# First cache pages and tables asked for later, and value loads in four portions, in the step kernel of a hybrid decoder

## The chip, the cores and the metric

The kernel runs on one core of one Trainium2 chip. The metric is the device time of one execution in microseconds (us). The core has five engines that run side by side and wait for each other by semaphores: TensorE (PE, matrix products), VectorE (DVE), ScalarE (ACT), GpSimd (POOL) and SyncE (SP). SP, ACT and POOL also issue transfers (DMAs), which 16 DMA engines carry out.

## What is computed

One layer of a decoder step for a prompt of 512 tokens (after 16 learned meta tokens) and for 8 sampled sequences of 8 new tokens with 1024 past positions each. The part that matters here, from the reference:

```python
xn = rmsnorm(hs, norm1[l])
qa, ka, va, qkv_b, z, b_raw, a_raw = project(xn, w_in[l], q_norm[l], k_norm[l])
kpast = cache_k[l][page_table].reshape(db, n_past, HA, 2, DQK)
vpast = cache_v[l][page_table].reshape(db, n_past, HA, DVA)
oa = diff_attn_core(qa, k_all, v_all, qpos, kpos, ..., lam, slopes)       # 4 heads
gq, gk, gv, gg, gbeta, conv_new = gdn_inputs(qkv_b, state_conv[l], ...)   # causal conv, 4 taps
s_new, ob = gdn_chunk(state_ssm[l].astype(f32), gq, gk, gv, gg, gbeta)    # 4 heads
hs = hs + merge_heads(oa, ob, z, ...)
hs = hs + peer_ffn(rmsnorm(hs, norm2[l]), ...)                            # 128 experts a token
```

The prompt goes through the same functions. All values are 32-bit floats.

## The kernel before

The 592 tokens lie in five tiles: four of 128 prompt tokens and a last one of 80 rows (64 sample rows, 16 meta rows), which comes first (`ORDER`).

**Projection units.** The 3584 columns of the input projection are cut into seven sections of 512. A unit (`UNITS`) is one tile times one section: 8 products of 128x512, in four quarters of two. Units 0 to 2 are v, k and q of the sample tile; units 3 to 7 are the first conv section over all five tiles, 8 to 12 the second, and so on. The weights of a unit come in four pieces of 512 KB, into a ring of six buffers (`w_loads`, L668): piece 6 and later each wait for the quarter that used the buffer, so piece 15, the last quarter of unit 3, waits for the second quarter of unit 2.

**Conv steps.** Unit 3+m feeds conv step m. ACT copies the unit's result out (L989, which also frees its bank) and stores it to DRAM, SP loads its rows back shifted by the four taps (`conv_inputs`, L693 to L696), DVE multiplies and adds (L1397, L1399, L1400), ACT takes SiLU and squares (L1090, L1100). For steps 0 to 9 DVE then writes a mean square (L1407), POOL turns it into a norm factor (`conv_rstd`, L869), and DVE multiplies by it (L1412 or L1414), which SP spills (L705).

**Past attention.** The 8 sequences go in four pairs. For a pair, SP loads 16 pages of keys (`key_loads`, L815, 256 KB each) and POOL 16 pages of values (`value_loads`, L906). The buffers of values are `vtok`, `kT` and two parts of `zone`, four pages each, and are free again when the values of the pair in front are used up (`s_dpv`). The chain of pair p is: scores on PE (L2018, L2023), bias adds on DVE (L1591, L1592), maximum (L1595), exponential on ACT (L1214), factors on DVE (L1599 to L1601), weights turned on PE (L2033), copied by ACT (L1219), values weighted on PE (L2045, L2048). `small_columns` (L1774, L1776) are sixteen narrow products in the middle of the first pair's chain: they use the banks that its scores stand in, so they wait for the bias adds (`s_dadd`), and for the tables.

**What sets the order.** Every engine runs a queue in program order. That order is written by streams: each piece of work yields a due time, and `advance` always takes the one that is due first. Due times are no times of the chip; they order instructions. For the early part all are `early_at(k)`, directly or by `unit_at(n)` (10.4 a unit for units 4 to 14), `conv_at(m)` (unit 3+m, its length, plus 13), `past_at(p, k)` and `gdn_at(u, k)`. So the units are the filler between the steps of the pairs' chains, and a due time that is moved changes which instruction stands ahead of which.

```python
def advance(streams, until):
    while min(s.due for s in streams) <= until:
        s = min(streams, key=lambda s: s.due)
        s.due = next(s.steps, NEVER)
```

After the last unit the kernel routes each prompt tile to experts and gathers their rows (`peer_uv`), from about 500 us to the end. The functions that the change touches, with the line numbers of the profile:

## Time and profile before

| what | value |
|---|---|
| median of 3 runs | 2113.99 us (2113.4 to 2118.76) |
| the profiled execution | 2111.61 us, span 2109.9 us |
| PE, DVE, ACT, POOL busy | 81%, 63%, 38%, 37% of the span |
| mean traffic over the span | 369 GB/s |
| PE waits in the first 560 us for DVE L1601 (ahead of L2033) | 20.2 us in 4 waits, the longest 8.8 |
| PE waits there for weight pieces (ahead of L1763) | 19.8 us in 8 waits, the longest 13.3 |

The span is the time from the first to the last instruction of the profiled execution; the device time contains 1.7 us more. Views that cut the span into stretches give for each the busy time of each engine, the TensorE clock that was granted (1.00 is full speed, 2.4 GHz, 0.50 is 1.2 GHz) and the share of time in which the DMA engines were busy (it can come out a little above 1). A timeline lists instructions or merged runs of them in order; square brackets tell how long the engine was idle ahead of a row and what released it. The trace has two records for each product of `bank<-sb_w,sb_xnT`, the program's order has one row entry for it: x20 in a timeline are ten products.

### The profile page before, as it was taken

The numbers are of one execution on the slowest core, as the hardware profiler recorded it, in microseconds if no ns is written. First come the engines' busy times: TensorE is split into PE (matmuls) and PEld (weight loads), VectorE is DVE, ScalarE is ACT, GpSimd is POOL, SyncE is SP. The second block draws the span as 40 slices with busy tenths as digits, with TensorE's granted clock in tenths as the row PEclk, the third lists the DMA queues.
The fourth block names the chain that finished last, engine by engine and source line by source line (L and its number), as shares of the span: only waits on it lengthen the run. The fifth ranks groups of instructions, "written<-read, shape, count | busy, mean of one in ns | idle before, by whom it ended". The sixth has DMA issues, their size and how long they took to land.

```text
span 2109.9 us, 20560 instructions
## 1 busy us (share of the span) xinstructions
PE 1713.4 (81%) x6211; PEld 863.1 (41%) x6211; DVE 1333.7 (63%) x3023; ACT 801.0 (38%) x2371; POOL 778.8 (37%) x704
## 2 busy tenths in 40 slices
PE   5889799988897878889797879978895567776877
PEld 1333364547453445445344535443551223442211
DVE  1343514344797657887665888865787866669554
ACT  1342321231545523563533455453243332323433
POOL 3123010111344543436334444634433554444442
PEclk9889899999999999999898999999898879888999
DMA  9999633128899999999999999999999999999997
GB/s 331 325 348 340 223 116 112 48 100 325 354 426 415 427 428 428 426 419 413 426 407 427 427 426 403 419 414 426 427 426 411 427 428 427 428 426 427 427 427 318
DMA packets 137479, 779.61 MB, mean 369 GB/s; under 512 B 14863, under 2 KB 23839, under 8 KB 59784
## 3 DMA queue, kind: packets, MB, share of 16 engines
q0 software_dynamic: 88384, 621.30, 70.6%
q1 hardware_dynamic: 45504, 149.69, 18.9%
q10 hardware_dynamic: 3480, 7.31, 0.9%
q8 instruction: 49, 0.80, 0.1%
q14 instruction: 62, 0.51, 0.1%
HBM read 762.27 MB, written 16.26 MB: 369 GB/s over the span
## 4 chain that ended last, share of the span: by engine, by line
PE 36%; DMA 32%; DVE 16%; ACT 7%; issue 4%; POOL 2%; SPq 1%; POOLq 1%; ACTq 0%; another core or an unknown queue 0%; DVEq 0%
DMA sb_uv<-in_peer_uv,sb_eidx 28%; PE bank L2145 17%; DVE sb_uv L1742 7%; PE bank L1763 6%; PE bank L2112 3%; PE bank L2080 2%; DMA sb_hres<-pre_conv 1%; ACT sb_diag L1321 1%; DVE sb_hres L1716 1%; POOL sb_uv L948 1%; ACT sb_ew L1314 1%; ACT L1310 1%; PE bank L1877 1%; PE bank L1889 1%; DVE sb_top L1643 1%
## 5 line engine op out<-in xcount | busy, mean ns | idle before, releaser
L2145 PE MATMUL bank<-sb_uv,sb_diag 128*128 128x512 f32 (+1 forms) x1860 | 960.1, 653 | 308.5 <-ACT sb_diag L1321 296.5
L948 POOL DMA_INDIRECT sb_uv<-in_peer_uv,sb_eidx x576 | 685.0, 1189 | 903.1 <-PE bank L2145 695.4
L1742 DVE CUSTOM_DVE_ANT_0 sb_uv<-sb_uv,sb_xn 128x1024 f32<-128x1024 f32 x576 | 698.9, 1221 | 326.2 <-DMA sb_uv<-in_peer_uv,sb_eidx 316.4
L2145 PEld LDWEIGHTS bank<-sb_uv,sb_diag 128*128 128x128 f32 (+1 forms) x1860 | 338.5, 197 | 806.2 <-ACT sb_diag L1321 470.2
L1310 ACT ACTIVATE sb_gel<-sb_h 128x1 f32<-128x1 f32 x576 | 116.3, 202 | 796.4 <-DVE sb_h L1742 790.0
L1763 PE MATMUL bank<-sb_w,sb_xnT 128*128 128x512 f32 (+1 forms) x560 | 270.9, 626 | 32.7 <-DMA sb_w<-in_w_sections 19.8
L1321 ACT ACTIVATE sb_diag<-sb_stay,sb_ew 128x128 f32<-128x128 f32 (+1 forms) x465 | 183.2, 394 | 48.5 <-PE bank L2145 5.3
L1314 ACT ACTIVATE sb_ew<-sb_gel,sb_gate 128x1 f32<-128x1 f32 x576 | 169.7, 295 | 19.8
L2112 PEld LDWEIGHTS bank<-sb_rT,sb_zone 128*128 128x128 f32 x1280 | 156.8, 196 | 28.3 <-issue 28.3
L1763 PEld LDWEIGHTS bank<-sb_w,sb_xnT 128*128 128x128 f32 (+1 forms) x560 | 99.5, 189 | 157.3 <-issue 121.9
L2112 PE MATMUL bank<-sb_rT,sb_zone 128*128 128x128 f32 x1280 | 157.8, 279 | 1.8 <-issue 1.8
L1716 DVE SCALAR_TENSOR_TENSOR sb_hres<-sb_uv,sb_ew,sb_hres 128x1024 f32<-128x1024 f32 x111 | 142.2, 1281 | 0.2 <-ACT sb_ew L1314 0.2
L2080 PE MATMUL bank<-sb_zone,sb_rT 128*128 128x512 f32 x160 | 71.4, 593 | 2.0 <-ACT sb_rT L1247 2.0
L884 POOL TENSOR_TENSOR sb_rstd<-sb_ms,sb_minus_half 128x8 f32<-128x8 f32 (+1 forms) x10 | 16.4, 1642 | 104.4 <-DVE sb_ms L1425 104.3
L1742 DVE DVE_READ_ACCUMULATOR2_ANT sb_h<- 128x1 f32 x576 | 47.2, 82 | 0.0
L2080 PEld LDWEIGHTS bank<-sb_zone,sb_rT 128*128 128x128 f32 x160 | 30.2, 190 | 40.3 <-issue 40.3
L1397 DVE TENSOR_TENSOR sb_xin<-sb_xin,sb_taps 128x2048 f32<-128x2048 f32 (+1 forms) x8 | 18.3, 2289 | 39.3 <-DMA sb_xin<-pre_conv 39.3
L1310 ACT ACT_TABLE_LOAD x33 | 42.3, 1283 | 0.6
L1647 DVE FIND_INDEX8 sb_tix<-sb_top,sb_score 128x8 uint32<-128x128 f32 x144 | 38.4, 284 | 0.0
L1643 DVE MAX8 sb_top<-sb_score 128x8 f32<-128x128 f32 x144 | 31.4, 279 | 6.9 <-ACT sb_score L1282 6.9
L1489 DVE TENSOR_TENSOR sb_X<-sb_X,bank 128x256 f32<-128x256 f32 (+1 forms) x36 | 14.7, 408 | 29.7 <-PE bank L1889 28.1
L1877 PEld LDWEIGHTS bank<-sb_X,sb_MT 128*128 128x128 f32 (+1 forms) x184 | 23.0, 186 | 16.6 <-issue 16.2
(335 smaller groups left out, 1518.0 us busy)
## 6 DMA issues: line engine op xcount, KB each, us to landing
sb_zone<-in_w_route SPq DMA_DIRECT2D x20, 2304.0 KB
sb_w<-in_w_sections SPq DMA_DIRECT2D x40, 512.0 KB, 8.7
sb_zone<-in_w_mixer SPq DMA_DIRECT2D x10, 2048.0 KB
sb_uv<-in_peer_uv,sb_eidx POOLq DMA_INDIRECT x576
sb_sS<-in_cache_kT SPq DMA_DIRECT2D x32, 256.0 KB, 4.5
sb_zone<-in_cache_v POOLq DMA_DIRECT2D x32, 256.0 KB, 5.9
sb_zone<-in_cache_kT SPq DMA_DIRECT2D x32, 256.0 KB, 3.7
sb_hres<-pre_conv SPq DMA_DIRECT2D x6, 1024.0 KB
```

The lines of the kernel that those rows point to most:

```text
L948: nc.gpsimd.indirect_dma_start(uv[:, m % RING, :], None, i["peer_uv"], bass.IndirectOffsetOnAxis(ap=eidx[:, t % 2, n:n + 1], axis=0)).then ...
L1310: nc.scalar.activation(G["gel"][:, at], G["h"][:, at], ACT.Gelu).then_inc(s_dg, 1)
L1314: nc.scalar.activation(G["ew"][:, at], G["gel"][:, at], ACT.Copy, scale=gate[:, t % 2, n:n + 1]).then_inc(s_dg, 1)
L1321: nc.scalar.activation(G["diag"][:, d % DIAGS, 0:cols], eye, ACT.Copy, scale=G["ew"][:, at]).then_inc(s_dg, 1)
L1643: n_top = count.inc(nc.vector.max(top[:, q, k:k + 8], sets[q]), s_tk)
L1716: nc.vector.scalar_tensor_tensor(hres[:, t % 2, :], uv[:, m % RING, D:2 * D], G["ew"][:, m % 8:m % 8 + 1], hres[:, t % 2, :], ALU.mult, AL ...
L1742: nc.vector.tensor_tensor_reduce(out=uv[:, m % RING, 0:D], in0=uv[:, m % RING, 0:D], in1=xn2[:, t % 2, :], scale=1.0, scalar=0.0, op0=ALU. ...
L1763: ins = nc.tensor.matmul(bank[b][0:rows, :], lhsT=xT(t)[:, kk, :], rhs=F["w"][:, piece % PIECES, kk % 2, :], start=kk == 0, stop=kk == KC - 1)
L1877: ins = nc.tensor.matmul(bank[PAIR_BANKS[pair][0]][0:rows, n * rows:(n + 1) * rows], lhsT=B["MT"][0:rows, lv % 2, h, 0:rows], rhs=B["X"][0 ...
L2080: ins = nc.tensor.matmul(bank[6 + half][:, :], lhsT=R["rT"][:, k, :], rhs=weights_half(half)[:, k, :], start=k == 0, stop=k == KC - 1)
L2112: ins = nc.tensor.matmul(bank[6 + g % 2][:, 128 * s:128 * s + 128], lhsT=weights_half(g)[:, k, 128 * s:128 * s + 128], rhs=R["rT"][:, k, : ...
L2145: ins = nc.tensor.matmul(bank[half][0:rows, :], lhsT=G["diag"][:, d % DIAGS, 0:rows], rhs=uv[:, m % RING, D + 512 * half:D + 512 * half + ...
```

## The change

Only due times change, and the value loads get four due times in place of two:

- all four pairs: `past_at(p, k)` is 78 + 30 p + k in place of 66 + 32 p + k, so the first pair's steps come 12 later, the second's 10, the third's 8, the fourth's 6;
- the first pair's keys are due at 47 and 56 in place of 38.5 and 39.5, its values at 60, 64, 69 and 73 in place of 42 (two) and 51 (two);
- values of later pairs are due at 30, 32, 34 and 36 behind the pair in front, in place of 27 and 28;
- the biases are due at 62 in place of 46, the narrow weights and the two tables at 64, 66 and 70 in place of 54, 56 and 59;
- L1412/L1414 of a conv step and its spill come 1.1 later; `gdn_at` of the first two tiles starts 3 and 2 later.

```diff
 def gdn_at(u, k):
     if u < 2:
-        return early_at((208, 302)[u] + (2.06, 2.15)[u] * k)
+        return early_at((211, 304)[u] + (2.06, 2.15)[u] * k)
...
 def past_at(p, k):
-    return early_at(66 + 32 * p + k)
+    return early_at(78 + 30 * p + k)
...
-                    yield early_at(54)
+                    yield early_at(64)
                     sp.dma_start(F["wba"][:, :, :], i["w_ba"]).then_inc(s_tables, 16)
...
                 def past_biases():
-                    yield early_at(46)
+                    yield early_at(62)
...
                 def key_loads(p):
                     for half in range(2):
-                        yield past_at(p - 1, 5 + 2 * half) if p else early_at(38.5 + half)
+                        yield past_at(p - 1, 5 + 2 * half) if p else early_at(47 + 9 * half)
...
                 def value_loads(p):
                     for half in range(2):
-                        yield past_at(p - 1, 27 + half) if p else early_at(42 + 9 * half)
+                        yield past_at(p - 1, 30 + 4 * half) if p else early_at(60 + 9 * half)
                         if p == 0 and half == 0:
                             pool.wait_ge(s_vecs, 112)
                         for seq in range(2):
+                            if seq:
+                                yield past_at(p - 1, 32 + 4 * half) if p else early_at(64 + 9 * half)
...
-                        yield conv_at(m) + 8.5
+                        yield conv_at(m) + 9.6
                         dve.wait_ge(s_brs, m + 1)
```

Two lines are added, so in the changed kernel every line behind L896 has a number higher by 2.

**SP's queue, at the first key pages.** Here `sb_w` are the weight pieces, L638 a tile of x, L723 the stores of the sample tile's keys, L811 the reading of a page number, with which each load of a page begins. Before:

```order
L640 DMA sb_xin<-in_x_sample 64x1024
L641 DMA sb_xin<-in_meta_tokens 16x1024
L668 DMA sb_w<-in_w_sections 128x1024 x11
L811 TENSOR_LOAD sb_pages
L811 ISA x2
```

Now:

```order
L668 DMA sb_w<-in_w_sections 128x1024 x12
L723 DMA out_k_sample<-sb_qkn 64x512
L723 DMA out_k_prompt<-sb_qkn 16x512
L668 DMA sb_w<-in_w_sections 128x1024
L638 DMA sb_hres<-in_x_prompt 128x1024
L668 DMA sb_w<-in_w_sections 128x1024
L811 TENSOR_LOAD sb_pages
```

Piece 15, three stores and loads and pieces 16 and 17 now stand ahead of the first key page; before, eight key pages stood ahead of piece 15. The second eight key pages, which stood behind piece 15, now stand behind conv step 0's rows (L693, L694), and the biases and tables behind those.

**PE's queue, around the first pair's scores.** L1763 are the units, L2018 and L2023 the scores, L1774 and L1776 the small columns, L2033 the turned weights of the pair. Before:

```order
L1793 MATMUL bank<-sb_stay,sb_qkn 128x80 x8
L1763 MATMUL bank<-sb_w,sb_xnT 128x512 x10
L2018 MATMUL bank<-sb_sS,sb_qt 32x512 x8
L1763 MATMUL bank<-sb_w,sb_xnT 128x512 x2
L2018 MATMUL bank<-sb_zone,sb_qt 32x512 x8
L2023 MATMUL bank<-sb_kT,sb_qt 32x64 x8
L1763 MATMUL bank<-sb_w,sb_xnT 128x512 x8
L1774 MATMUL bank<-sb_xnT,sb_wba 8x512 x2
```

Now (line numbers higher by 2):

```order
L1795 MATMUL bank<-sb_stay,sb_qkn 128x80 x8
L1765 MATMUL bank<-sb_w,sb_xnT 128x512 x18
L2020 MATMUL bank<-sb_sS,sb_qt 32x512 x8
L1765 MATMUL bank<-sb_w,sb_xnT 128x512 x4
L2020 MATMUL bank<-sb_zone,sb_qt 32x512 x8
L2025 MATMUL bank<-sb_kT,sb_qt 32x64 x8
L1765 MATMUL bank<-sb_w,sb_xnT 128x512 x6
L1776 MATMUL bank<-sb_xnT,sb_wba 8x512 x2
```

From the turns of the sample tile to the small columns there stood 20 unit products, now 28; up to the end of the first pair's values 26, now 34. Between the pairs it is 24 and 24 (first to second), 24 and 24, then 24 and now 20.

**DVE's queue, between conv step 0 and the first pair's bias adds.** L1407, L1412 and L1397 to L1400 belong to conv steps, L1339 scales the last tile of turned x, L1346 is a mean square of a tile of x. Before:

```order
L1407 TENSOR_SCALAR sb_bms<-sb_bss 80x4
L1339 TENSOR_TENSOR sb_xnT<-sb_xnT,sb_gain 128x1024
L1591 TENSOR_TENSOR sb_pot<-bank,sb_bias_past 128x512 x2
L1592 TENSOR_TENSOR sb_pot<-bank,sb_oT 128x64
L1412 SCALAR_TENSOR_TENSOR sb_kqv<-sb_kqv,sb_brs 80x512
```

Now (line numbers higher by 2):

```order
L1409 TENSOR_SCALAR sb_bms<-sb_bss 80x4
L1341 TENSOR_TENSOR sb_xnT<-sb_xnT,sb_gain 128x1024
L1414 SCALAR_TENSOR_TENSOR sb_kqv<-sb_kqv,sb_brs 80x512
L1348 TENSOR_SCALAR sb_ms<-sb_ss 128x1 x2
L1399 TENSOR_TENSOR sb_hres<-sb_hres,sb_taps 128x2048
L1401 TENSOR_TENSOR sb_hres<-sb_hres 128x1024
L1402 TENSOR_TENSOR sb_hres<-sb_hres 128x512
L1593 TENSOR_TENSOR sb_pot<-bank,sb_bias_past 128x512 x2
```

The adds now stand behind the norm of step 0 and all of conv step 1. In POOL's queue the norm factors L869 stood one ahead of the second pair's 16 value loads (besides the sample tile's) and three behind; now it is three ahead and three behind. The third pair's loads had one sample-tile and two prompt-tile factors behind them and now have two behind them; of the fourth pair's, four stand ahead of the last factor and twelve behind it, where all 16 stood ahead of the last two. The first pair's four portions now have one L860 or L869 or both between them, and the third portion stands behind the L860 that waits for the DVE row L1346 behind conv step 0.

## Rows read from the trace of the kernel before

**Rows 1.** Stretches: span of each, then busy us (instructions), clock, DMA share, GB/s

```profile
25.00:59.00 34.00, 16.74 (x32) 4.78 (x33) 7.05 (x14) 1.90 (x3) 12.01 (x18) 0.81 1.03 396
59.00:104.30 45.30, 41.22 (x196) 16.58 (x195) 17.25 (x30) 19.61 (x51) 6.06 (x6) 0.95 0.92 316
104.30:150.80 46.50, 37.06 (x158) 15.64 (x157) 19.74 (x32) 18.56 (x53) 11.70 (x19) 0.85 0.96 352
150.80:193.40 42.60, 39.37 (x185) 17.47 (x185) 18.11 (x24) 16.24 (x48) 11.69 (x19) 0.92 0.89 308
193.40:238.40 45.00, 35.94 (x151) 14.70 (x150) 21.41 (x23) 11.95 (x30) 11.20 (x19) 0.85 0.77 285
260.00:440.00 180.00, 172.88 (x763) 98.33 (x762) 64.20 (x117) 39.48 (x93) 17.16 (x13) 0.99 0.28 92
```

**Rows 2.** Timeline of PE, start: start us, us, what, records, [idle before, releaser]

```profile
26.60 5.51 PE L1763 MATMUL bank<-sb_w,sb_xnT 128*80 128x512 f32 x12 [2.39 <-DMA sb_w<-in_w_sections]
...
55.52 3.70 PE L1763 MATMUL bank<-sb_w,sb_xnT 128*80 128x512 f32 x4 [13.34 <-DMA sb_w<-in_w_sections]
...
62.62 10.52 PE L1763 MATMUL bank<-sb_w,sb_xnT 128*128 128x512 f32 x20 [2.06 <-issue]
```

**Rows 3.** Timeline of SP's queue

```profile
5.31 23.56 SPq L668 DMA_DIRECT2D sb_w<-in_w_sections  x11
35.36 6.28 SPq L815 DMA_DIRECT2D sb_sS<-in_cache_kT  x8
41.68 0.44 SPq L668 DMA_DIRECT2D sb_w<-in_w_sections  x1
```

**Rows 4.** The page's DMA issues: operation, count, KB each, median us to landing

```profile
sb_w<-in_w_sections SPq DMA_DIRECT2D x40, 512.0 KB, 8.7
...
sb_zone<-in_cache_v POOLq DMA_DIRECT2D x32, 256.0 KB, 5.9
```

**Rows 5.** The chain of waits in the first 520 us: start us, us, what

```profile
41.68 13.80 DMA sb_w<-in_w_sections
```

**Rows 6.** Timeline of PE, the four pairs

```profile
86.58 1.03 PE L1774 MATMUL bank<-sb_xnT,sb_wba 128*8 128x512 f32 x4 [0.53 <-DVE sb_pot L1592]
...
92.81 2.00 PE L2033 MATMUL bank<-sb_pot 128*128 128x64 f32 x16 [0.16 <-DVE sb_pot L1601]
...
135.81 3.68 PE L2033 MATMUL bank<-sb_pot 128*128 128x64 f32 x16 [8.78 <-DVE sb_pot L1601]
...
139.83 6.38 PE L1763 MATMUL bank<-sb_w,sb_xnT 128*128 128x512 f32 x8
...
181.51 2.52 PE L2033 MATMUL bank<-sb_pot 128*128 128x64 f32 x16 [3.23 <-DVE sb_pot L1601]
...
209.20 8.85 PE L1763 MATMUL bank<-sb_w,sb_xnT 128*128 128x512 f32 x20
226.06 3.67 PE L2033 MATMUL bank<-sb_pot 128*128 128x64 f32 x16 [8.01 <-DVE sb_pot L1601]
```

**Rows 7.** Timeline of DVE, conv steps and bias adds

```profile
77.63 2.29 DVE L1397 TENSOR_TENSOR sb_xin<-sb_xin,sb_taps 80x2048 f32<-80x2048 f32 x1 [11.53 <-DMA sb_xin<-pre_conv]
...
85.11 1.28 DVE L1591 TENSOR_TENSOR sb_pot<-bank,sb_bias_past 128x512 f32<-128x512 f32 x2
...
127.12 1.28 DVE L1591 TENSOR_TENSOR sb_pot<-bank,sb_bias_past 128x512 f32<-128x512 f32 x2
...
256.33 2.29 DVE L1397 TENSOR_TENSOR sb_hres<-sb_hres,sb_taps 128x2048 f32<-128x2048 f32 x1 [4.30 <-DMA sb_hres<-pre_conv]
```

**Rows 8.** Timeline of POOL, the second pair's values

```profile
104.97 2.29 POOL L906 DMA_DIRECT2D sb_vtok<-in_cache_v  x4 [4.76 <-PE bank L2048]
...
121.26 1.04 POOL L869 TENSOR_TENSOR sb_brs<-sb_bms,sb_minus_half 128x4 f32<-128x4 f32 x1
```

**Rows 9.** The DMA queues from 42 to 56 us: packets, MB, share of 16 engines

```profile
q1 hardware_dynamic: 1618, 3.21, 61.7%
q0 software_dynamic: 702, 2.27, 42.1%
```

More of the change, by code:

```diff
@@ L647, in tables_loads @@
                     sp.dma_start(st("ident"), stay_table[:, 0:128]).then_inc(s_ident, 16)
-                    yield early_at(54)
+                    yield early_at(64)
                     sp.dma_start(F["wba"][:, :, :], i["w_ba"]).then_inc(s_tables, 16)
-                    yield early_at(56)
+                    yield early_at(66)
                     sp.dma_start(stay[:, 128:], stay_table[:, 128:]).then_inc(s_tables, 16)
-                    yield early_at(59)
+                    yield early_at(70)
                     sp.dma_start(F["early"][:, :], early_table).then_inc(s_tables, 16)
@@ L698, in spills @@
                 def spills(m):
-                    yield conv_at(m) + (9.5 if m < 2 * NT else 4.7)
+                    yield conv_at(m) + (10.6 if m < 2 * NT else 4.7)
                     sec, n = divmod(m, NT)
```

## The prediction

> **What bounds the kernel now.** I read the stretches first [rows 1]. From 260 us on PE is busy 172.88 of 180 us and the DMA engines 0.28 of the time; there and later the change moves only a few products. Before 238.4 us it is the other way round: the DMA engines are at 1.03 up to 59 us and at 0.92, 0.96, 0.89 and 0.77 in the stretches that end with each pair's values, while PE idles and its clock falls to 0.81 and 0.85. So the early part is bound by two things at once: transfers nearly all the time, and PE waits at single places. PE's timeline names the places. One is at 42.18 us: PE waits 13.34 us for a weight piece [rows 2]. The others are waits for DVE L1601 ahead of L2033, 8.78, 3.23 and 8.01 us in pairs two to four [rows 6]. Each costs more than itself. Behind the first wait a quarter of a unit takes 3.70 us; at full clock a record takes 8.85 / 20 = 0.44 us, a quarter 1.8 [rows 2, 6]. A gap that closes at PE before 240 us moves everything behind it, since PE is full afterwards.
>
> **The sum, against the profiled execution (2111.61 us).**
>
> A, the weight piece. SP issues piece 15 at 41.68, straight behind eight key pages that took it from 35.36, and it lands 13.80 us later [rows 3, 5]. It needs only the second quarter of unit 2, which is two thirds through the run that starts at 26.60: about 30.3 [rows 2]. In the new order the piece stands with its eleven forerunners, so it is issued at about 30.4 and lands between 30.4 + 8.7 (the median) and 30.4 + 13.8: 39.1 to 44.2 [rows 4, 5]. PE comes for it at 55.52 - 13.34 = 42.18. The wait falls to 0 to 2 us; I take 0.3, a gain of 13, since the value pages that shared the engines are gone too. The clock adds 3.70 - 1.8 for that quarter and 10.52 - 8.85 for the next run [rows 2, 6]: 3.5. Of the 2.39 us ahead of 26.60 and the like I take 1. A = 17.5 (11 to 21).
>
> B, the first pair. DVE gets conv step 0's rows at 77.63 and does the adds at 85.11, 7.5 us later [rows 7]. Now the adds stand behind the norm of step 0 and all of step 1. From the rows at time T: about 4.3 for step 0 on DVE, 0.6 for the tile's factor on POOL, 4.1 for the third portion of values (a quarter of the 16.3 us from 104.97 to 121.26), only then 1.0 for L869 of step 0, then on DVE 0.7 for L1412, 4.3 for step 1 and 2.6 for the adds: 17.6, and 1.4 for seven handovers, T + 19 [rows 7, 8]. T itself moves with A: 77.6 - 17.5 = 60.1, so the small columns can start at 79.3. PE reaches them earlier: units restart at 62.62 - 17.5 = 45.1, then 28 products of 0.885 and 4.2 us of scores: 74.1 [rows 2, 6]. A new wait of 5.2 us, where 0.53, 0.16 and about 1 us stood [rows 6]. B = -4 (0 to -10). Behind PE there only units are queued; DVE, ACT and POOL don't wait for them in this stretch. The fourth portion of values is issued by T + 17.6 = 77.7 and lands 5.9 later [rows 4]; PE wants it after 91. Tables and biases are issued about as long ahead of their use as before. Both cost nothing while that cover of some 7 us stands; without it PE would wait the same at L2045.
>
> C, the second pair. Before, its 16 value loads held POOL from 104.97, L869 came at 121.26, and DVE, in order, did the adds at 127.12. The scores were ready before 120: PE stood at L2033 from 135.81 - 8.78 = 127.03, behind eight products of filler, 7.1 us [rows 6 to 8]. Now three L869 stand ahead of the loads. But the next L869 stands behind all 16, and the L1412 that waits for it stands between the pair's maximum and its L1599. By my walk the loads start late, behind the third L869, and that L1412 comes some 7 us after PE's filler of ten products is through. The 8.78 us stall stays for the most part, and with it the slow clock (3.68 against 2.00, 6.38 against 3.6 [rows 6]). C = 2, between 0 and 13.2 (all of it gone).
>
> D, the third pair: no L869 is waited for between adds and L1601 now. The wait of 3.23, 0.5 us at L2033 and some 3 us of slow clock behind it are at stake [rows 6]. D = 5 (0 to 7.5).
>
> E, the fourth: the adds stand behind one operation of a conv step in place of three, and POOL issues four loads ahead of the last L869, not 16. At stake are 8.01, 1.7 and about 1.8 us [rows 6]. E = 7 (0 to 11.5).
>
> F, the first delta-net tile: L1456 stands behind all of conv step 13, whose rows came at 256.33 [rows 7]; now its L1399 and L1400 (1.9 us) stand ahead too, and PE arrives sooner relative to rows that take as long as before. F = -3 (0 to -8).
>
> A to F give 24.5. **But the transfers must fit.** The same pages, pieces and rows must land before each pair. DMA engines idle 8% of 45.3, 4% of 46.5, 11% of 42.6 and 23% of 45 us [rows 1]: 3.6 + 1.9 + 4.7 + 10.4 = 20.6 us, all there is to squeeze out up to 238.4 us. And the change makes new idle time. Eight key pages leave SP's queue at 35.36 and eight value pages POOL's about then: 4.2 MB, or 10.6 us at 396 GB/s, and until piece 16, x and the pages follow there is less to fetch [rows 1, 3]. Most of the hole is filled by what comes next; I take 3 us as lost. The cap is 20.6 - 3 = 17.6, and I forecast a gain of **17 us**: 2094.6 against 2111.61; the median of the runs is 2.4 above the profiled execution, so 2097.
>
> A rule of the skill that speaks against this. From 42 to 56 us SP's ring (q1) had 61.7% of the engines' time and POOL's (q0) 42.1% [rows 9]: with both at work SP's got about three fifths. The Trainium skill (DMA: Bandwidth & Descriptors, Queues, rings and completion order) says that each DMA engine goes round robin between the queue rows that have work, a packet at a time, and takes one row's descriptors in ring order. By that conv step 0's rows would wait behind the key pages in SP's ring and T would follow A only with that ring drained. Without the rule the sum is 24.5, with it 13.5; the same mechanism, worked out from rows alone, is the first rival.
>
> **The rivals.**
>
> 1. SP's ring holds the rows back. From about 36 to 46 us SP issues 5.8 MB (pieces 16 and 17, eight pages, three tiles of x, the taps) ahead of step 0's rows; before, those rows went out behind a similar load with ten more microseconds to drain. At three fifths of 396 GB/s, 238 GB/s, the ring has moved 3.1 MB when the rows are queued at 49, and the rest takes 11 us [rows 1, 9]. T is then about 71, the small columns wait 16 us, and 11 of A's 17.5 are lost; rows of later steps go through the same ring, which costs half of D and E. For it: the shares. Against it: in that time POOL has four pages to issue and then waits. 24.5 - 11 - 6 is a gain of 7.5, 2106.5.
>
> 2. The transfers take it back: pairs three and four keep their waits (D and E zero), because rows of conv steps land late in a queue that is full. That leaves A + B + C + F = 12.5 at most, and no less than the 3.6 + 1.9 - 3 = 2.5 us of idle DMA time up to 150.8; the middle is a gain of 7.5, 2106.5.
>
> 3. More fits than I allow: no new idle time, and weights and rows are not needed as early relative to PE. All of 24.5: 2089.5. For it: the last stretch has 23% idle, and the fourth pair has 20 unit products ahead where 24 stood.
>
> 4. Slower. T doesn't move at all: row loads are issued earlier but land at 77.6. PE then stands at the small columns from 74 to 77.6 + 19 = 96.8, where it entered them at 86.58 with eight products (7.1 us) less done [rows 6]. That is 10.2 - 7.1 = 3.1 us behind, and 23 us of idle time cost about 2 us of slow clock, as at 55.52 [rows 2]. C, D, E zero, F -3: 3.1 + 2 + 3 is 8 us slower, 2122. It decides where T comes down by less than about 5 us, so 73 and above. Against it: A moves the store of unit 3 by 17 us, and nothing but the ring lies between.
>
> That the change doesn't do what it says is excluded for A: the order shows the piece ahead of the pages, and its only other wait is over at 30.3.
>
> **How the numbers follow.** The forecast (2092 to 2102) gets 0.52. Rivals 1 and 2 get 0.13 and 0.12: their time lies at the bound of 0.3% (6.3 us, about what a measurement of this kernel can tell from no change), so of the 0.25 about half goes to faster, half to same. Rival 3 gets 0.14, rival 4 0.07; 0.02 is left for a small shift that nets nothing. Faster: 0.52 + 0.14 + 0.12 = 0.78. Same: 0.13 + 0.02 = 0.15. Slower 0.07. The range leaves out rival 4 and the tail of rival 3: 2086 to 2110.
>
> **What would show it.** Right: piece 15 issued near 30.4, PE's wait at 42 us under 2; step 0's rows on DVE near 60; a wait of about 5 us ahead of the small columns on DVE L1592 (two lines on in the new file), still 6 to 9 us at the second pair, under 2 at the third and fourth; the fourth pair's values used up 15 to 20 us before 238.4; DMA share at 0.93 or more up to there; the stretch after 260 us as long as before. Wrong: rows on DVE after 70 (rivals 1 and 4); waits at pairs three and four as before (rival 2); or a change behind 260 us, which I cost at nothing since PE's filler there is nearly the same.

## The result and the profile after

The changed kernel takes 2123.34 us (median of 20 runs, 2116.69 to 2134.19) where the kernel before takes 2118.51 (20 runs on the same chip): a ratio of 1.0027, interval 1.0015 to 1.0038, some 6 us slower. The forecast was 17 us faster. Its profiled execution took 2120.38 us with a span of 2118.7, against 2111.61 and 2109.9.

The stretches of the changed kernel, cut where each pair's values are used up (columns as in [rows 1]):

```profile
25.00:59.00 34.00, 31.05 (x82) 12.09 (x84) 8.31 (x16) 9.14 (x19) 9.18 (x11) 1.00 1.03 405
59.00:109.60 50.60, 34.59 (x168) 12.65 (x168) 20.97 (x33) 15.60 (x46) 9.14 (x14) 0.83 0.98 344
109.60:154.30 44.70, 35.92 (x156) 15.28 (x156) 19.83 (x32) 18.68 (x53) 11.72 (x19) 0.85 0.92 324
154.30:204.60 50.30, 38.41 (x187) 16.96 (x185) 18.48 (x24) 16.37 (x48) 11.72 (x19) 0.86 0.82 303
204.60:242.90 38.30, 32.21 (x143) 13.99 (x143) 20.70 (x21) 9.47 (x20) 10.26 (x18) 0.87 0.69 240
260.00:440.00 180.00, 167.55 (x743) 95.89 (x740) 61.13 (x113) 39.88 (x86) 15.91 (x11) 0.98 0.28 90
```

From 25 to 59 us PE is busy 31.05 us, where it was busy 16.74. The ends are 109.6, 154.3, 204.6 and 242.9 where [rows 1] has 104.3, 150.8, 193.4 and 238.4. The last row has 5.3 us less of PE than before, in a stretch that I had costed at nothing.

PE's timeline of the changed kernel, with the places that waited:

```profile
29.08 10.84 PE L1765 MATMUL bank<-sb_w,sb_xnT 128*80 128x512 f32 x24 [0.17 <-DMA sb_w<-in_w_sections]
...
70.83 3.64 PE L2020 MATMUL bank<-sb_zone,sb_qt 128*32 128x512 f32 x16 [6.33 <-DMA sb_zone<-in_cache_kT]
...
90.46 1.88 PE L1776 MATMUL bank<-sb_xnT,sb_wba 128*8 128x512 f32 x4 [9.68 <-DVE sb_pot L1594]
...
140.55 3.68 PE L2035 MATMUL bank<-sb_pot 128*128 128x64 f32 x16 [8.78 <-DVE sb_pot L1603]
...
179.96 1.89 PE L2035 MATMUL bank<-sb_pot 128*128 128x64 f32 x16
194.00 6.03 PE L1765 MATMUL bank<-sb_w,sb_xnT 128*80 128x512 f32 x8 [11.89 <-DMA sb_w<-in_w_sections]
```

The 13.34 us at the weight piece [rows 2] are 0.17. In their place stand 6.33 for the second half of the first keys and 9.68 ahead of the small columns. The second pair waits 8.78 as before; the third pair's 3.23 are gone, but 11.89 for a weight piece come behind it.

**Where the time went, in one scale.** The change moves unit products past the pairs, so equal points of the program don't have equal work behind them. I take from a point's start 0.885 us (two records of 8.85 / 20 us, [rows 6]) for each unit product that stands ahead of it in PE's order. What is left is how late the rest is:

| point | before | changed | later by |
|---|---|---|---|
| end of unit 3 (L1793; 32 products ahead in both) | 59.01 - 28.32 = 30.7 | 39.76 - 28.32 = 11.4 | -19.2 |
| small columns (52; 60 ahead) | 40.6 | 37.4 | -3.2 |
| first values used (58; 66) | 51.9 | 50.1 | -1.8 |
| second (82; 90) | 77.1 | 73.6 | -3.5 |
| third (106; 114) | 98.6 | 102.7 | 4.1 |
| fourth (130; 134) | 122.4 | 123.2 | 0.8 |
| first delta-net tile (146; 148) | 125.1 | 126.0 | 0.9 |
| its first operand, L1862 (154; 156) | 132.1 | 138.6 | 6.5 |
| L2071, near 470 us (280; 280) | 217.2 | 223.8 | 6.6 |

A second profiled execution of the changed kernel (below) has 11.9, 37.1, 48.8, 73.9, 101.1, 121.4, 124.2, 136.1 and 221.3. So a single number is good to 2 or 3 us, and not always: two kernels below whose orders are the same up to the second values have 76.4 and 71.3 there. Three things stand out. Of the 19 us, 16 are gone by the small columns. The third pair loses 7.6 more (5.8 in the second execution), of which the fourth gives back 3.3 (3.6), so that at the tile the changed kernel is level with the one before: 0.9 later in one execution, 0.9 sooner in the other. And the last 5 to 6 us, all that the runs show, come in one step behind 257 us.

That step on DVE, in the changed kernel:

```profile
258.35 1.22 DVE L1401 TENSOR_TENSOR sb_hres<-sb_hres 128x1024 f32<-128x1024 f32 x1
...
262.54 0.48 DVE L1464 COPY sb_wq<-bank 128x320 f32<-128x320 f32 x1
270.59 2.29 DVE L1399 TENSOR_TENSOR sb_xin<-sb_xin,sb_taps 128x2048 f32<-128x2048 f32 x1 [7.57 <-DMA sb_xin<-pre_conv]
272.92 0.88 DVE L1470 TENSOR_TENSOR sb_APT<-bank,sb_DT 80x320 f32<-80x320 f32 x2
...
276.09 0.49 DVE L1475 TENSOR_TENSOR sb_XT<-sb_stay,sb_MT 80x320 f32<-80x320 f32 x1
```

and in the kernel before:

```profile
265.13 0.88 DVE L1468 TENSOR_TENSOR sb_APT<-bank,sb_DT 80x320 f32<-80x320 f32 x2 [1.80 <-PE bank L1857]
266.05 0.49 DVE L1472 TENSOR_TENSOR sb_MT<-sb_APT,sb_early 80x320 f32<-80x320 f32 x1
266.57 0.49 DVE L1473 TENSOR_TENSOR sb_XT<-sb_stay,sb_MT 80x320 f32<-80x320 f32 x1
268.93 2.29 DVE L1397 TENSOR_TENSOR sb_xin<-sb_xin,sb_taps 128x2048 f32<-128x2048 f32 x1 [1.87 <-DMA sb_xin<-pre_conv]
```

With the tile's start 3 later (211 for 208), the product of conv step 14 goes ahead of the tile's masked products. DVE stands 7.57 us at rows that aren't there, the ready operand behind it, and PE waits 7.95 us for that at L1864.

### The profile page after: what moved, and what is told of

The parts are those of the page before. It is cut to its first block, busy times and chain, and to the rows that moved or that the text cites. A ratio compares the mean times of both kernels' runs of the same rounds, so it can differ in the third digit from the quotient of the medians.

```text
span 2118.7 us, 20557 instructions
## 1 busy us (share of the span) xinstructions
PE 1707.2 (81%) x6211; PEld 860.5 (41%) x6211; DVE 1334.2 (63%) x3023; ACT 802.1 (38%) x2371; POOL 780.0 (37%) x704
## 4 chain that ended last, share of the span: by engine, by line
PE 34%; DMA 32%; DVE 17%; issue 7%; ACT 7%; POOL 2%; SPq 1%; POOLq 1%; another core or an unknown queue 0%; ACTq 0%; DVEq 0%
DMA sb_uv<-in_peer_uv,sb_eidx 29%; PE bank L2147 15%; DVE sb_uv L1744 7%; PE bank L1765 7%; PE bank L2114 2%; PE bank L2082 2%; DVE sb_hres L1718 1%; POOL sb_uv L950 1%; DMA sb_hres<-pre_conv 1%; ACT sb_diag L1323 1%; ACT sb_ew L1316 1%; ACT L1312 1%; PE bank L1879 1%; DVE sb_tix L1649 1%; DMA sb_xin<-pre_conv 1%
## 5 line engine op out<-in xcount | busy, mean ns | idle before, releaser
L869 POOL TENSOR_TENSOR sb_brs<-sb_bms,sb_minus_half 128x4 f32<-128x4 f32 (+1 forms) x10 | 10.2, 1020 | 78.4 <-DVE sb_bms L1409 78.3
L1649 DVE FIND_INDEX8 sb_tix<-sb_top,sb_score 128x8 uint32<-128x128 f32 x144 | 38.5, 288 | 0.0
```

The source lines that it names most:

```text
L1649: n_used = count.inc(nc.vector.max_index(tix[:, q, k:k + 8], top[:, q, k:k + 8], sets[q]), s_cut if k and q == quads[-1] else s_tk)
```

## The experiments

Ratios are against the kernel before on the same chip, with a 95% interval; "late" is the scale of the table above. Two theories. **Order:** PE stands behind an engine that stands, in its fixed order, at something else that is late. **Capacity:** the transfers are the bound, and what is won in one place is given back.

### The step behind 257 us

The starts of both tiles go back in the changed kernel, and the same edit is made alone, the other way round, in the kernel before:

```diff
-        return early_at((211, 304)[u] + (2.06, 2.15)[u] * k)
+        return early_at((208, 302)[u] + (2.06, 2.15)[u] * k)
```

> The changed kernel with the first two delta-net tiles' starts as before (208 and 302 for 211 and 304), so that DVE has the masked products of the first tile (L1470 to L1475) ahead of conv step 14's product L1399 again. Order theory (the loss behind 260 us is DVE standing at rows that are not there, with PE's operand queued behind them): PE's wait of 7.95 us at L1864 on DVE L1475 falls below 2 us, and since PE is full afterwards the whole kernel gains 6 to 8 us: 0.2 to 0.3% faster than before. Capacity theory (the early part is bound by transfers and what is won in one place is given back in the next): PE waits as long at a neighbouring place, the stretch from 260 to 440 us stays where it is, and the time stays within 2 us of the changed kernel's, 0.2 to 0.3% slower than before.

Measured: 1.0017 (1.0002 to 1.0032). PE's wait at L1864 is gone, and L1862 and L2071 stand at 131.8 and 216.9 in the scale, as in the kernel before (132.1, 217.2). But the kernel is not 0.2 to 0.3% faster than before; it is still 0.17% slower, at the edge of the interval.

> The kernel before with one part of the change alone: the first two delta-net tiles' starts at 211 and 304 (for 208 and 302). On DVE the sums of conv step 13 go ahead of the tile's first operations and conv step 14's product ahead of its masked products; PE and SP up to 238 us are untouched. If the loss behind 260 us is this order alone: PE waits 6 to 8 us for the operand made by L1473, and the kernel is 5 to 8 us slower than before (0.25 to 0.4%), as much as the whole change costs. If it takes the other parts too (late rows, shifted units): the wait is under 2 us and the time within 0.1% of before.

Measured: 1.0026 (1.0009 to 1.0043), the whole cost of the change, though PE's wait was 3.51 us and its L2071 3.4 later than before in the profiled execution. DVE's row of conv step 14 in that kernel, ahead of the masked products:

```profile
268.67 2.53 DVE L1397 TENSOR_TENSOR sb_xin<-sb_xin,sb_taps 128x2048 f32<-128x2048 f32 x1 [4.20 <-DMA sb_xin<-pre_conv]
```

> The changed kernel as it is, as the yardstick for the kernels beside it on this chip. Both theories: 0.2 to 0.4% slower than before; PE's wait of 8 us at L1864 is there again; 70 to 77 MB have been moved by 240 us, as before.

Measured: 1.0032 (1.0015 to 1.0050); the wait at L1864 is 7.9 again. Made alone, the later tile starts cost what the change costs. Undone, they give back 0.10 to 0.15% of the 0.27 to 0.32%, which the intervals don't tell from all of it nor from nothing; it is the trace that shows PE level with the kernel before from L1862 to L2071. That only the first tile's start matters and not the second's is read from the table (6.5 later at L1862, 6.6 at L2071), since no run moves one of them alone.

### Where the 19 us went: the first pair

The weight piece alone, in the kernel before:

```diff
-                        yield past_at(p - 1, 5 + 2 * half) if p else early_at(38.5 + half)
+                        yield past_at(p - 1, 5 + 2 * half) if p else early_at(39.6 + half)
```

> The kernel before with one edit: the first pair's key pages due at 39.6 and 40.6 in place of 38.5 and 39.5, so that weight piece 15 goes ahead of them; pages, tables, values and all later dates stay. Order theory: PE's wait of 13.34 us at 42.18 goes, units 2 and 3 end some 15 us sooner, and since all that follows keeps its old place in the queues, 4 to 10 us of that reach 238.4 us: 0.2 to 0.5% faster than before. Capacity theory: the eight key pages and everything behind them land as before, conv step 0's rows still reach DVE near 77, and the first pair's values are used up within 2 us of 104.3: no difference from before.

Measured: 1.0008 (0.9991 to 1.0024). Unit 3 ends at 41.92, 17 us sooner, and the small columns come at 86.31 where they came at 86.58. PE's wait only moved:

```profile
PE bank L1774 <- DVE sb_pot L1592: 15.6, 1, 15.6
```

So the piece alone was worth nothing: DVE has conv step 0's rows at 77.36, where it had them at 77.63 [rows 7], and does the adds 7.5 us later as before. The first 80 us of the kernel before and of the changed one (columns as in [rows 1]):

```profile
0.00:80.00 80.00, 51.14 (x147) 17.68 (x148) 11.85 (x21) 12.24 (x23) 19.81 (x37) 0.89 0.99 347
```

```profile
0.00:80.00 80.00, 62.33 (x175) 23.08 (x176) 15.84 (x28) 16.92 (x37) 20.18 (x37) 0.96 0.99 349
```

PE did 11 us more, but the engines moved 347 x 80 = 27.8 MB before and 27.9 MB after, at a share of 0.99. Up to here I take transfers to be the bound; that is read from the share, and no run took bytes out of this stretch. Two edits change only who comes first. The key pages behind the rows of conv step 0:

```diff
-                        yield past_at(p - 1, 5 + 2 * half) if p else early_at(47 + 9 * half)
+                        yield past_at(p - 1, 5 + 2 * half) if p else early_at(54.8 + 1.2 * half)
```

> The changed kernel with the first pair's first eight key pages issued behind conv step 0's rows and two tiles of x on SP, where they stood ahead of them. If these pages in SP's own queue hold the rows (the first rival of the prediction): 2.1 MB less stand ahead of them, and the rows reach DVE 4 to 8 us before 65.5, with the first keys later than PE wants them at 61 by 3 to 8 us. If the rows wait for something else (the store of the unit, the value pages in POOL's queue): they reach DVE within 2 us of 65.5, and only the loss at the keys is left. The kernel's time: within 5 us of the changed kernel's in both.

Measured: 1.0074 (1.0052 to 1.0096). The rows in the changed kernel and in this one:

```profile
65.53 2.29 DVE L1399 TENSOR_TENSOR sb_xin<-sb_xin,sb_taps 80x2048 f32<-80x2048 f32 x1 [18.73 <-DMA sb_xin<-pre_conv]
...
84.79 2.29 DVE L1399 TENSOR_TENSOR sb_hres<-sb_hres,sb_taps 128x2048 f32<-128x2048 f32 x1 [7.88 <-DMA sb_hres<-pre_conv]
```

```profile
60.02 2.29 DVE L1399 TENSOR_TENSOR sb_xin<-sb_xin,sb_taps 80x2048 f32<-80x2048 f32 x1 [12.96 <-DMA sb_xin<-pre_conv]
...
89.43 2.29 DVE L1399 TENSOR_TENSOR sb_hres<-sb_hres,sb_taps 128x2048 f32<-128x2048 f32 x1 [10.05 <-DMA sb_hres<-pre_conv]
```

With 2.1 MB less ahead of them in SP's queue the rows come 5.5 us sooner, at 60.02, where the prediction had them (60.1). The Trainium skill (DMA: Bandwidth & Descriptors, Queues, rings and completion order) has a DMA engine take one queue row's descriptors in ring order. The 5.5 us agree with that; they don't prove it, since 2.1 MB at 396 GB/s are 5.3 us, and pages taken from another queue might have given the same. But PE now waits 5.13 and 2.70 us for keys, step 1's rows come 4.6 us later, and the kernel loses. Conv step 1's rows ahead of the tables:

```diff
-                    yield early_at(62)
+                    yield early_at(70.6)
                     sp.dma_start(bias_past[:, :], past_table[:, 0:PAST]).then_inc(s_pg, 16)
...
-                    yield early_at(64)
+                    yield early_at(71)
...
-                    yield early_at(66)
+                    yield early_at(71.5)
...
-                    yield early_at(70)
+                    yield early_at(72)
```

> The changed kernel with the biases and the three tables issued behind conv step 1's row load on SP instead of ahead of it; nothing else moves. Queue-order theory (the rows reach DVE 19 us after their issue because 1.3 MB more of tables and pages stand ahead of them in SP's ring): the rows reach DVE 3 to 6 us sooner than 84.8, PE's wait of 9.68 us for the adds L1594 falls to 4 to 6 us, and the first pair's values are used up some 4 to 6 us before 109.6. What is left of that at 243 us tells how much the later pairs take back: all of it by the capacity theory (time as the changed kernel's, within 1 us), 3 to 6 us by the order theory.

Measured: 1.0062 (1.0042 to 1.0082). The small columns' wait fell to 2.4, the first values were used at 45.4 in the scale (50.1 in the changed kernel), and at the second pair 77.9 stands against 73.6: PE waited 12.0 us there. Winning 5 us at the first pair made the later ones worse: 130.6 at the delta-net tile against 126.0. The trace tells why in part: conv step 3's factor came 2.4 us later on POOL (118.84 for 116.41), and the second pair's loads stand behind it.

### Does capacity bind the second pair?

In both kernels the second pair's keys and values at a quarter of their width, 6.3 MB less:

```diff
+                                wide = HW // 4 if p == 1 else HW
-                                pool.dma_start(cache_quarter(k)[:, g, :], ...)
+                                pool.dma_start(cache_quarter(k)[:, g, 0:wide], ...)
```

(and the keys on SP likewise; the second pair's results are then not those of the layer)

> The changed kernel with the second pair's 16 key and 16 value pages loaded at a quarter of their width (6.3 MB less to move up to 150 us, some 16 us at 396 GB/s; the columns left out keep what the first pair left there); all instructions, waits and orders stay. Capacity theory: the second pair's values are used up 8 to 16 us before 154.3, since all transfers of that stretch were queued one behind the other. Order theory (PE stands behind DVE, and DVE behind rows and factors that come late for their place in the queues): PE's wait at the second pair stays above 5 us, and its values are used up less than 5 us before 154.3. Between both (rows of conv steps are late because they share the queues with pages): the rows of conv steps 3 to 5 reach DVE some us sooner and the gain is 4 to 8.

> The kernel before with the same quarter-wide pages of the second pair. It tells how much the kernel before is held by transfers in the same stretch: by the capacity theory its second pair's values are used up 8 to 16 us before 150.8, by the order theory less than 5 (POOL's loads still stand ahead of L869, and their issue takes the same 16 us).

Measured in one execution each, late at the second values: 70.7 in the changed kernel (73.6), 76.9 in the one before (77.1). The two rows for 80 to 160 us, changed and changed with small pages:

```profile
80.00:160.00 80.00, 61.54 (x282) 25.92 (x281) 37.85 (x58) 33.17 (x93) 16.22 (x26) 0.85 0.91 320
```

```profile
80.00:160.00 80.00, 63.37 (x301) 27.87 (x300) 39.14 (x62) 35.16 (x102) 16.71 (x27) 0.87 0.73 241
```

The share falls from 0.91 to 0.73 and PE's wait at L2035 is still 7.38 us (9.84 in the kernel before). The 8 to 16 us of the capacity theory are not there. At the second pair order binds for the most part; a share of 0.9 proved nothing.

### Which order

POOL's factor of conv step 4 between the second pair's loads:

```diff
-                        yield past_at(p - 1, 30 + 4 * half) if p else early_at(60 + 9 * half)
+                        yield past_at(p - 1, 30 + (9 if p == 1 else 4) * half) if p else early_at(60 + 9 * half)
```

(and 32 + 4 * half likewise)

> The changed kernel with the second pair's third and fourth portions of values due 5 later (117 and 119 for 112 and 114), so that POOL computes conv step 4's factor (L869) between the second and the third portion rather than behind the fourth. Order theory: DVE's wait of 9.69 us at L1414 falls to about 1, PE's wait of 8.78 us at L2035 for L1603 falls below 2, and the clock behind it (3.68 us for a record group that takes 2.0 at full clock) is back: the second pair's values are used up 8 to 12 us before 154.3. Capacity theory: PE reaches the value products earlier but waits there for pages of cache_v by as much as it gained, and 154.3 moves by less than 3 us. In both, what the kernel's time shows is smaller than what is won at 154.3, if the wait for a weight piece in the third pair (11.89 us at 188) grows by it.

Measured: 1.0067 (1.0046 to 1.0088). DVE in the changed kernel, and with the edit:

```profile
136.92 0.69 DVE L1414 SCALAR_TENSOR_TENSOR sb_cs<-sb_cs,sb_brs 128x512 f32<-128x512 f32 x1 [9.69 <-POOL sb_brs L869]
```

```profile
127.17 0.69 DVE L1414 SCALAR_TENSOR_TENSOR sb_cs<-sb_cs,sb_brs 128x512 f32<-128x512 f32 x1 [1.33 <-POOL sb_brs L869]
136.56 2.29 DVE L1399 TENSOR_TENSOR sb_hres<-sb_hres,sb_taps 80x2048 f32<-80x2048 f32 x1 [8.70 <-DMA sb_hres<-pre_conv]
```

The wait for POOL went and the next in the queue, for conv step 5's rows, had always stood behind it. Both theories missed this. So the turn was made on DVE itself, at three places:

```diff
+SOONER = {(0, 5): 78.2, (1, 12): 118.9, (3, 5): 171.8, (3, 7.5): 171.85, (3, 9): 171.88, (3, 12): 171.95}
+def fold_at(p, k):
+    return early_at(SOONER[p, k]) if (p, k) in SOONER else past_at(p, k)
...
-                    yield past_at(p, 12)
+                    yield fold_at(p, 12)
```

(the same for the adds, the maximum and the exponential; in these kernels the lines behind 228 have numbers 7 higher than in the changed one: the units are L1772, the weight pieces L675)

> The changed kernel with DVE's order turned at three places: the first pair's adds ahead of conv step 1's product, the second pair's folding (L1601 to L1603) ahead of conv step 4's factor and step 5's product, and the fourth pair's adds, maximum, exponential (ACT) and folding ahead of conv step 10's product. No transfer is issued elsewhere. Order theory (PE's waits of 9.7, 8.8 and 6.1 us are DVE standing at rows or factors that aren't there): all three fall below 2 us, with the clock behind them, and the kernel gains 8 to 15 us on the changed kernel, which is 0.1 to 0.5% faster than before. Capacity theory (the DMA engines move the same 53.5 MB up to 160 us and 76.7 MB up to 240 us in every kernel so far): the waits go, and PE waits as long for pages or weights a little further on; the places where the second and the fourth pair's values are used up move by less than 4 us, and the time by less than 3 us.

Measured: 1.0001 (0.9987 to 1.0014). The small columns are 9 us less late, the second pair's folded weights (L2033 before) 7, but at the second values 76.4 stands (73.6): the waits came back at the next step, 11.2 us for ACT's copy of those weights, queued behind conv step 5's rows. Its profiled execution is the slowest of its twelve, so the gain against the changed kernel (1.0032 on this chip) rests on the runs. With the old tile starts as well:

> The changed kernel with the three turns of DVE's order (adds and folding of pairs one, two and four ahead of conv steps) and the delta-net tiles' old starts (208 and 302), but with the value loads at the changed kernel's dates. Each of the two gained 0.15 to 0.3% on the changed kernel by itself, at places that have nothing to do with each other. If they add up: 0.1 to 0.4% faster than before. If the turned order only shifts waits to the next instruction of the same queue, nothing more than the delta-net part is left: within 0.1% of before or 0.1 to 0.2% slower.

Measured: 0.9983 (0.9968 to 0.9999), faster than both kernels; 120.2 in the scale at the tile and 210.8 at L2071 (before 125.1 and 217.2). At the second values, up to which its orders are those of the kernel above, it has 71.3.

### The late weight piece of the third pair

> The changed kernel with the value loads of the third and fourth pair at their old absolute dates (125 and 126, 157 and 158), ahead of two factors (L869) on POOL behind which they stand in the changed kernel; nothing else moves. Theory of the late pages (POOL waits 17.5 us for conv step 6's factor while the DMA engines are at 0.64, then keys, values and weights come at once and the weight piece lands 14 us after its issue): the loads are issued near 156 in place of 166, the DMA share from 160 to 180 goes from 0.64 to above 0.85, PE's wait of 11.9 us at 188 for the piece falls below 4, and the third pair's values are used up 6 to 9 us before 204.6; at the fourth pair some 3 us of that are left. Rival (weights, not pages, are what is late: SP issues the piece only when PE has freed its buffer): the wait stays above 8 us. The kernel's time: 1 to 4 us less than the changed kernel's.

Measured: 1.0132 (1.0110 to 1.0153), 21 us slower than the changed kernel by the ratios and 25 by the medians, where I had expected 1 to 4 faster. The wait for a weight piece in the third pair did fall, from 11.89 to 4.14 us. But POOL took the loads ahead of two factors and waited 19.08 us for their buffers, and DVE stood behind it:

```profile
157.34 2.29 POOL L908 DMA_DIRECT2D sb_vtok<-in_cache_v  x4 [19.08 <-PE bank L2050]
...
173.60 1.03 POOL L869 TENSOR_TENSOR sb_brs<-sb_bms,sb_minus_half 80x4 f32<-80x4 f32 x1
```

```profile
174.67 0.69 DVE L1416 TENSOR_TENSOR sb_kqv<-sb_kqv,sb_brs 80x512 f32<-80x512 f32 x1 [28.78 <-POOL sb_brs L869]
```

So the change's later loads are worth much once the pairs are later. This edit with the turns and the old starts:

> The changed kernel with the three turns of DVE's order, the third and fourth pair's value loads at their old dates, and the first two delta-net tiles' starts as before (208 and 302). Order theory: the sum of its parts, 15 to 25 us less than the changed kernel, 0.5 to 0.9% faster than before. Capacity theory: only the 7 us of the delta-net tile and 2 to 4 of the later pages: 4 to 6 us less than before at most, within 0.3% of it.

Measured: 1.0044 (1.0031 to 1.0056); the bad part outweighs the good ones. On the 0.9983 kernel, half of the third pair's loads go into POOL's gap between two factors:

```diff
-                        yield past_at(p - 1, 30 + 4 * half) if p else early_at(60 + 9 * half)
+                        yield past_at(p - 1, 29.2 if p == 2 and not half else 30 + 4 * half) if p else early_at(60 + 9 * half)
```

(and 29.3 for 32 likewise)

> The same base kernel with the first half of the third pair's value loads between conv step 5's and step 6's factor on POOL, which waits 17.8 us there for rows while the DMA engines are at 0.72. The other eight stay behind step 6's factor, so nothing waits longer for POOL (with all sixteen ahead it cost 25 us). Late-pages theory: the weight piece that landed 14 us after its issue lands after 8 to 10, PE's wait of 12 us for it falls to 6 to 8, and the time falls by 2 to 5 us. If the keys in SP's own queue hold the piece: the wait stays above 10 and the time within 2 us.

Measured: **0.9954** (0.9940 to 0.9969). The piece in the kernel it comes from, and here:

```profile
176.20 0.52 SPq L675 DMA_DIRECT2D sb_w<-in_w_sections  x1
```

```profile
191.79 6.48 PE L1772 MATMUL bank<-sb_w,sb_xnT 128*80 128x512 f32 x8 [11.98 <-DMA sb_w<-in_w_sections]
```

```profile
176.46 0.52 SPq L675 DMA_DIRECT2D sb_w<-in_w_sections  x1
```

```profile
186.72 5.91 PE L1772 MATMUL bank<-sb_w,sb_xnT 128*80 128x512 f32 x8 [6.56 <-DMA sb_w<-in_w_sections]
```

Issued at the same time it was there after 10.3 instead of 15.6 us, while the DMA engines did the first eight pages in a stretch with idle time: from 150 to 170 us their share is 0.88 for 0.62. It is 5.7 us less late at the third values (95.2 for 100.9), and at L2071 still 6.1.

### How far it goes

> The kernel with the turned sums and the old delta-net starts (0.17% faster than before), with also the first pair's maximum, factor of the output, exponential and folding ahead of conv step 1 on DVE and ACT, and the second pair's copy of the folded weights (ACT) ahead of conv step 5. Order theory: PE's waits of 8.3 us (first folding) and 6.9 us (for that copy, ahead of the second pair's values) go; of 15 us a third to two thirds reach 240 us: 5 to 10 us, 0.4 to 0.6% faster than before. Capacity theory: PE waits for the first pair's value pages (4.0 us so far) and the second pair's by what it gained: within 2 us of the kernel it comes from.

Measured: 0.9979 (0.9962 to 0.9996). The first folding comes 10 us less late (32.2 for 42.0), the first values only 1.6. At them PE now waits 5.87 us, and not for pages but for ACT's copy of the folded weights, which stands in ACT's queue behind conv step 2's SiLU:

```profile
98.24 0.63 ACT L1099 ACTIVATE sb_cs<-sb_xin 128x512 f32<-128x512 f32 x1 [4.50 <-DVE sb_xin L1409]
...
101.79 0.20 ACT L1229 ACTIVATE sb_pot<-bank 64x64 f32<-64x64 f32 x1
```

The wait for value pages, 10.27 us, is at the second pair. POOL issues that pair's first pages at 121.11, behind a factor for which it stood 16.46 us, and the last four from 135.07. So this too is order, on ACT and on POOL, at least as much as capacity.

> Both edits on the same base kernel. If the waits are orders and independent: the sum of the two gains, 0.5 to 0.8% faster than before. If transfers bind once the orders are right: no more than the better of the two, and PE's remaining waits up to 240 us are for pages and weights.

Measured: 0.9952 (0.9936 to 0.9968), the better of the two and no more. PE waits 7.49 us for ACT's copy at the first values and 9.65 for pages at the second.

> The best kernel so far (0.48% faster than before) with the fourth portion of the first pair's values issued on POOL some 5 us sooner, ahead of conv step 0's factor and one tile's factor. If PE's wait of 9.7 us for value pages is set by their late issue: it falls to 5 to 7, at the price of conv step 0's factor 2.5 us later, which DVE has room for; a gain of 1 to 3 us. If transfers bind there (share 1.04 from 40 to 80 us): the pages land as late as before, and nothing changes by more than 1 us.

Measured: 0.9957 (0.9939 to 0.9975). The wait fell to 7.8, and 3.0 us came at the small columns: nothing. I had read the 9.7 us as a wait of the first pair. It is the second pair's, and at the first values PE waits 7.36 us for ACT's copy, so this run says little about when the first pair's pages land.

> The kernel before, with weight piece 15 ahead of the first pair's key pages (due 39.6), the first pair's adds ahead of conv step 0's product and the folding of pairs two to four ahead of the conv steps' factors on DVE. If the orders alone are what matters, it gains as the changed kernel did by its turned sums and more, since nothing of the change's losses is there: PE's waits of 8.8, 3.2 and 8.0 us fall below 3, 0.3 to 0.6% faster than before. If later dates for pages are needed as well: PE waits for pages or for its bank instead, and the time is within 0.2% of before.

Measured: 0.9978 (0.9962 to 0.9995), with a new wait of 13.7 us ahead of the small columns. The adds ran 18 us sooner, at 67.35, but the small columns also need the last tile of turned x, and DVE scales it (L1339 before, L1346 here) behind conv step 0's rows, as late as before (84.22 for 83.98 us):

```profile
77.88 2.29 DVE L1404 TENSOR_TENSOR sb_xin<-sb_xin,sb_taps 80x2048 f32<-80x2048 f32 x1 [9.11 <-DMA sb_xin<-pre_conv]
...
84.22 1.21 DVE L1346 TENSOR_TENSOR sb_xnT<-sb_xnT,sb_gain 128x1024 f32<-128x1024 f32 x1
```

The turned orders are worth 0.2% here and 0.3% in the changed kernel (1.0001 against 1.0032). Whether the split loads would give their 0.3% to the kernel before too wasn't tried.

## Why the prediction was wrong, by its own steps

In the scale of the table A to F came out at 19.2, -17.4, 1.7, -7.6, 3.3 and -5.6, which is some 6.5 us slower in place of 24.5 faster (the forecast capped that at 17). B and D hold 26 of the 31 us between them.

- **A, the weight piece, 17.5: right as a mechanism**, 19.2 at the end of unit 3, the piece among its forerunners, the wait 0.17. It was counted as a gain of the kernel, and it is none (the run with the piece alone: 1.0008).
- **B, -4 (0 to -10): the step that failed first.** From 19.2 ahead at unit 3 to 3.2 ahead at the small columns and 1.8 at the first values it came out at -17.4 (-15.6 in the second execution). T was 65.5 where I had 60.1: the transfers ahead in SP's queue, which I had left to the first rival; with eight key pages taken from ahead of them the rows came at 60.0. T + 19 for the end of the adds took conv step 1's rows as there. They came at 84.8, behind eight key pages, x, biases and tables; DVE stood 7.88 us for them, and the small columns started at T + 24.9. That tables and biases cost nothing was argued for their own use only, not for the rows behind them in the same queue. The 6.33 us for the second half of the keys I hadn't named at all, nor the half clock through the small columns (1.88 and 1.92 us for what takes 1.03 [rows 6]). One slip went the other way: I counted 2.6 us for the adds, and in [rows 6, 7] the small columns start 1.5 us behind their start.
- **C, 2: right.** The wait is 8.78 to the hundredth, behind a factor of POOL behind sixteen loads; 1.7 in the scale (0.1 in the second execution).
- **D, 5: the second step that failed, wrong sign, -7.6.** The 3.23 us went (3.4 gained from the second values to L2033), and a weight piece issued between eight key pages and sixteen value pages came 11.89 us too late. The change had pushed these loads from 151 to 166 us, and I had asked only what the loads hold up on POOL, not what they collide with. Up to then the DMA engines had room (a share of 0.64 from 160 to 180 us, 0.92 before). In the kernel with turned orders, half of these loads issued from 153 us bring its wait of 11.98 down to 6.56.
- **E, 7: right in sign, half the size, 3.3.** Wait 8.01 to 6.09.
- **F, -3 (0 to -8): inside its range, mis-sized.** From the tile's start to its first operand it cost 5.6. I had named conv step 13's sums, which cost nothing (DVE's two copies behind them start at 262.13 and were at 262.44 before); the 7.57 us are conv step 14's product ahead of L1470, one place further on in the order.
- **The cap, 17.6: wrong use.** Idle shares say how much could be squeezed out, and nothing was: 0.99, 0.91 and 0.80 for 80 us each, against 0.99, 0.91 and 0.81. In the first 80 us PE did 11 us more and the bytes moved were the same; where the share was 0.9, much of the idle time was made by engines that wait in order.
- **Rivals.** The first had the mechanism for T that the runs fit, at twice its size: 11 us for 5.4. That its 71 + 19 = 90 for the small columns is the measured 90.5 is luck, since T was too late there and the rows of step 1 too early. The second, D zero, was nearest in its place, and too mild. The fourth, slower, was near in size (8 us slower; 5 to 6 measured), and that is luck: T moved by 12 us, where it had T stand still. Of what would show it wrong I had listed "a change behind 260 us"; that came.

What stays open: why the kernel with POOL's factor moved measures 0.35% (7 us) slower than the changed kernel. Against that one's second execution it is 0.7 less late at the second values, 1.3 more at L1862 and 4.0 at L2071; no wait in its trace answers to that.

## What to carry to other kernels

Follow a gain to the next point where two engines meet, and count what that point waits for: if it is a transfer and the DMA share up to there is 1, a piece that comes sooner may push another back, as here conv step 0's rows (5.5 us sooner) pushed step 1's (4.6 later). An instruction moved by a few units of due time is to be looked up on each in-order engine for what it now stands behind, the last place in the program as well as the first; here 3 in one due time at the far end costs as much as the whole change. And before loads are moved, ask both what they hold up on the issuing engine and what they will share the DMA engines with when they go: the best edit filled a gap of one engine and of the DMA engines at once.

## What was unexpected of the hardware

The slow clock came in full behind much shorter waits than those of 8 us and more from which I had its price; behind 3.23 us I had read only 2.52 us for what takes 2.00 [rows 6]. After 5.13 us for keys (the run with the rows ahead) and after 3.48 (the changed kernel's second execution) a group took 3.64 us that takes 1.92; after 2.70 us it took 2.54. But the 3.51 us at L1862 in the run with the tile's start alone were followed by four records in 0.48, which take 0.44. The wait's length alone doesn't tell it.

The clock also fell where PE did not wait. In the run with the weight piece alone (first row) its granted clock was 0.66 with PE busy all of the time, against 0.94 in the kernel before in the same stretch (second row):

```profile
330.00:360.00 30.00, 30.00 (x61) 10.90 (x60) 13.80 (x21) 4.60 (x18) 1.00 (x1) 0.66 0.26 74
```

```profile
330.00:360.00 30.00, 28.84 (x100) 13.44 (x99) 15.23 (x24) 8.45 (x25) 1.00 (x1) 0.94 0.35 105
```

The two kernels are the same there, level to 0.1 us at 268 us and 6.7 us apart at 470. Such stretches come in some executions and not in others, and are as large as what was to be measured here: the times of one kernel spread over 8 to 18 us, and with twelve runs of a kernel the interval is still 0.3% wide.
